# Retention and differential attention of block 1 in one run of 16 paired steps

## The reference

```python
scores = q @ k.T * 64 ** -0.5                       # retention, per head
dmask  = exp(lg_f * max(dist, 0)) * exp(lg_b * max(-dist, 0))
ret    = rms_norm((scores * dmask) @ v, g_ret) * silu(gate)
s      = q[m] @ k[m].T - slope[h] * abs(dist)       # differential, m = 0, 1
p      = softmax(s)
da     = rms_norm((p[0] - lam * p[1]) @ v, g_diff) * (1 - lam_init)
x      = x + concat(ret, da) @ w_out[l]
```

## Time and profile before

| | |
|---|---|
| median of 3 runs | 3374.51 us (3371.18 to 3377.08) |
| the profiled execution's own time | 3373.53 us |
| its span, first to last instruction | 3371.7 us |
| PE busy | 3133.2 us (93%) |
| PE weight loads | 2408.7 us (71%) |
| DVE busy | 1773.0 us (53%) |
| ACT busy | 1177.6 us (35%) |
| POOL busy | 1059.9 us (31%) |
| mean granted PE clock | 0.953 |

### The profile page before, as it was taken

The page is one execution under the profiler, slowest core; times in us unless marked ns, Lnnn a source line. Parts: engine busy times, 40 slices in busy tenths (PEclk is TensorE's granted clock), DMA queues, the critical chain, the costliest instruction groups (busy, mean ns, idle before and its releaser), DMA issues. The chain is left out here.

```text
span 3371.7 us, 45874 instructions
## 1 busy us (share of the span) xinstructions
PE 3133.2 (93%) x15912; PEld 2408.7 (71%) x15912; DVE 1773.0 (53%) x2788; ACT 1177.6 (35%) x1763; POOL 1059.9 (31%) x468
## 2 busy tenths in 40 slices
PE   7997699999999689999899898899999898899999
PEld 5842378887762268888678667788888676778787
DVE  4347764445436774445431674653354337657272
ACT  3224444233232535222222673332232225633231
POOL 3410144444330034444222313222223231144443
PEclk9988899999988789999999999999999898999999
DMA  4420034343340024444111001112122120023232
GB/s 147 148 80 0 23 124 150 127 151 111 126 140 0 0 89 148 131 148 133 50 50 56 29 28 50 44 62 75 50 65 72 43 69 21 1 81 101 86 99 94
DMA packets 72784, 270.06 MB, mean 80 GB/s; under 512 B 7920, under 2 KB 8944, under 8 KB 72560
## 3 DMA queue, kind: packets, MB, share of 16 engines
q1 hardware_dynamic: 71024, 264.34, 24.1%
q10 hardware_dynamic: 1664, 4.44, 0.4%
HBM read 266.65 MB, written 2.10 MB: 80 GB/s over the span
## 5 line engine op out<-in xcount | busy, mean ns | idle before, releaser
L524 POOL TENSOR_TENSOR w_lo<-w_raw,w_hi 128x1024 fp32r<-128x1024 f32 (+1 forms) x364 | 946.3, 2600 | 1559.9 <-ACT w_hi L1014 1559.9
L600 PE MATMUL ps<-h_hi,w_hi 128*128 128x512 f32 x3040 | 1040.7, 376 | 56.5 <-DVE h_lo L1530 29.5
L600 PE MATMUL ps<-h_lo,w_hi 128*128 128x512 f32 x3040 | 1025.8, 372 | 0.0
L600 PE MATMUL ps<-h_hi,w_lo 128*128 128x512 f32 x3040 | 1024.5, 371 | 0.0
L1014 ACT ACTIVATE w_hi<-w_raw 128x1024 fp32r<-128x1024 f32 (+1 forms) x364 | 406.4, 1117 | 1388.5 <-PE ps L600 1378.5
L600 PEld LDWEIGHTS ps<-h_hi,w_hi 128*128 128x128 f32 x3040 | 533.3, 190 | 188.9 <-issue 41.4
L600 PEld LDWEIGHTS ps<-h_hi,w_lo 128*128 128x128 f32 x3040 | 533.4, 191 | 100.6
L600 PEld LDWEIGHTS ps<-h_lo,w_hi 128*128 128x128 f32 x3040 | 534.3, 191 | 96.0 <-issue 0.5
L1659 DVE TENSOR_SCALAR conv_y<-u_pad,small 128x770 f32<-128x770 f32 (+1 forms) x88 | 176.2, 2002 | 196.8 <-ACT u_pad L1170 196.6
L1618 DVE SCALAR_TENSOR_TENSOR xT<-ps,mod,xT 128x512 f32 (+1 forms) x72 | 45.4, 659 | 309.9 <-PE ps L600 309.9
L1463 DVE CUSTOM_DVE_ANT_0 mod_junk<-mod_w,silu_c 128x1024 f32<-128x1024 f32 x96 | 140.8, 1467 | 121.7 <-DMA mod_w<-w_mod_dram 121.6
(11 more groups left out here) (192 smaller groups left out, 3488.4 us busy)
## 6 DMA issues: line engine op xcount, KB each, us to landing
mod_w<-w_mod_dram SPq DMA_DIRECT2D x96, 512.0 KB, 3.6
w_raw<-w_gu_dram SPq DMA_DIRECT2D x88, 512.0 KB, 3.5
w_raw<-w_down_dram SPq DMA_DIRECT2D x64, 704.0 KB, 4.1
w_raw<-w_up_dram SPq DMA_DIRECT2D x88, 512.0 KB, 3.4
w_raw<-w_in_dram SPq DMA_DIRECT2D x56, 512.0 KB, 3.5
w_raw<-na_qkv_dram SPq DMA_DIRECT2D x24, 512.0 KB, 3.5
w_raw<-w_out_dram SPq DMA_DIRECT2D x16, 512.0 KB, 3.5
w_raw<-swa_qkv_dram SPq DMA_DIRECT2D x12, 512.0 KB, 3.5
```

What stands on the lines that cost most here:

```text
L524: pool.tensor_tensor(w_lo[par][:, 0:cols], w_raw[par][:, 0:cols], w_hi[par][:, 0:cols].bitcast(F32), ALU.subtract).then_inc(w_lo_ready, 1)
L600: last = pe.matmul(acc[par][:, to:to + n], w[par][:, k * P:k * P + P], r[:, k, frm:frm + n], start=begin, stop=end)
```

## The change

The three phases become one, `mix`, of 16 steps s = 4 j + b over pair j and block b. Each step takes block b of both retention heads of pair j and query block b of differential head j. PE in step s scores the differential maps (banks 2, 3) and the retention heads (banks 0, 1), multiplies the retention values of s-1, turns s-2 and multiplies the differential values of s-3. The loops are unrolled, so q, k, v are read in `proj1` itself. The masks are made by three exponentials on ACT (384, 128 and 512 columns) and one product of 128 columns on POOL. DVE adds the bias and takes the minimum of the negated scores in one operation. Instead of dividing by both sums it forms e1 * lam * S0/S1 - e0, where e and S are a map's exponentials and their sum; the norm that follows cancels the remaining factor, if its epsilon is multiplied by S0 squared (`x_e2`) and the sign is turned in the gain. The squares and the gate product go to POOL. The means of all eight tiles are packed into few rows (`pack_tile`, 32 columns of weights), root and reciprocal are then taken of 128 x 128 twice in place of eight times 128 x 512, and `spread_tile` copies the rows back over the partitions by matmuls. The first `w_out` unit takes its tiles in the order 0, 1, 2, 4, 5, 3, 6, 7, with four of the spreads between its matmuls. The strip `d_dist` is loaded earlier, beside the other two, and some small buffers move to shared memory.

```diff
-        add("retention", layer=l)
-        add("diff", layer=l)
-        add("fin1", layer=l)
+        add("mix", layer=l)
...
-                    sp.dma_start(r_dpos[:], d["dist"][0]).then_inc(tab["retention"], 16)
-                    sp.dma_start(r_dneg[:], d["dist"][1]).then_inc(tab["retention"], 16)
+                    for n, strip in enumerate((r_dpos, r_dneg, d_dist)):
+                        sp.dma_start(strip[:], d["dist"][n]).then_inc(tab["mix"], 16)
...
+                def middle(j, hd):
+                    pool.wait_ge(x_strip, 8 * l + 2 * j + hd + 1)
+                    mask = r_mask[j % 2][hd][:, S - P:S]
+                    pool.tensor_tensor(mask, mask, r_mid[:, hd, :], ALU.mult).then_inc(x_mask, 1)
+
+                def square(n, tile, ready, count):
+                    pool.wait_ge(ready, count)
+                    if n >= 2:
+                        pool.wait_ge(f_sum, 32 * l + 4 * (n - 1))
+                    pool.tensor_tensor(f_sq[n % 2][:], proj1[:, tile, :], proj1[:, tile, :], ALU.mult
+                                       ).then_inc(f_sq_ready, 1)
+
+                def gate(j):
+                    pool.wait_ge(f_sq_ready, 7 * l + 2 * j + 1)
+                    pool.tensor_tensor(proj1[:, 8 + j, :], proj1[:, 8 + j, :], proj1[:, 24 + j, :], ALU.mult
+                                       ).then_inc(f_gated, 1)
...
+                def score_r(s):
+                    j, b = divmod(s, 4)
+                    if s:
+                        pe.wait_ge(x_masked, 32 * l + 2 * s)
+                    for hd, half in enumerate(halves_):
+                        pe.matmul(bank(hd), proj1[half, 12 + j, b * P:b * P + P], proj1[half, 8 + j, :],
+                                  start=True, stop=True).then_inc(x_scored, 1)
+
+                def score_d(s):
+                    j, b = divmod(s, 4)
+                    if s:
+                        pe.wait_ge(d_biased, 32 * l + 2 * s)
+                    for m, half in enumerate(halves_):
+                        pe.matmul(bank(2 + m), proj1[half, j, b * P:b * P + P], proj1[half, 4 + j, :],
+                                  start=True, stop=True).then_inc(d_scored, 1)
+
+                def values_r(s):
+                    j, b = divmod(s, 4)
+                    pe.wait_ge(x_masked, 32 * l + 2 * s + 2)
+                    if b == 0:
+                        pe.wait_ge(x_v_kept, 8 * l + 2 * j + 1)
+                        if j:
+                            pe.wait_ge(x_r_taken, 4 * l + j)
+                    for hd, half in enumerate(halves_):
+                        pe.matmul(bank(4)[half, :], r_vs[j % 2][:, b, half], r_sc[s % 2][:, hd, :],
+                                  start=(b == 0), stop=(b == 3)).then_inc(x_summed, 1)
...
+                    for c in range(4):
+                        last = pe.transpose(bank(6)[:, c * P:c * P + P], d_s[s % 3][:, 0, c * P:c * P + P], mat(IDENT))
+                    last.then_inc(d_turned, 1)
...
+                    for c in range(4):
+                        last = pe.matmul(bank(5)[:, b * P:b * P + P], d_vs[j % 2][:, c, :], d_aT[s % 2][:, c, :],
+                                         start=(c == 0), stop=(c == 3))
+                    last.then_inc(d_summed, 1)
...
+                    for g in range(4):
+                        last = pe.matmul(to[32 * g:32 * g + 32, 0:P], mats[:, PACKX, frm:frm + 32],
+                                         f_sq[n % 2][:, g * P:g * P + P], start=begin, stop=end and not which)
+                        if not which:
+                            last.then_inc(f_sum, 1)
+                    if which:
+                        pe.wait_ge(d_e2, 4 * l + j + 1)
+                        for g in range(4):
+                            pe.matmul(to[32 * g:32 * g + 32, 0:P], x_e2[j % 2][:, g, 14 - row:46 - row], mat(IDENT),
...
+                    for g in range(4):
+                        if which:
+                            at_ = 32 * g + row
+                            last = pe.matmul(to[:, g * P:g * P + P], mat(IDENT)[:, at_:at_ + 1].broadcast_to([P, P]),
+                                             x_rs[batch][:], start=True, stop=True)
+                        else:
+                            for hd, half in enumerate(halves_):
+                                at_ = 32 * g + row + hd
+                                last = pe.matmul(to[half, g * P:g * P + P],
+                                                 mat(IDENT)[:, at_:at_ + 1].broadcast_to([P, HD]),
...
+                turn_v(0)
+                turn_v(1)
+                for s in range(STEPS + 3):
+                    if s < STEPS:
+                        score_d(s)
+                        score_r(s)
+                    if 1 <= s <= STEPS:
+                        values_r(s - 1)
+                    if 2 <= s < STEPS + 2:
+                        turn_d(s - 2)
+                    if s >= 3:
+                        values_d(s - 3)
+                    if s < 12 and s % 4 >= 2:
+                        turn_v(2 * (s // 4) + s % 4)
+                    if s >= 6 and s % 2 == 0 and s < 18:
+                        pack_tile(s // 2 - 3)
+                for t in range(4):
+                    spread_tile(t)
+                pack_tile(6)
+                pack_tile(7)
+
+                def tail(at_):
+                    if at_ == 0:
+                        spread_tile(4)
+                    elif 2 <= at_ < 5:
+                        spread_tile(at_ + 3)
+                ends[0] = tail
 
             def na(ph):
...
+                    act.activation(mask[:, S:STRIP], r_dpos[:, S:STRIP], ACT.Exp, scale=lgam[:, at_:at_ + 1])
+                    act.activation(r_mid[:, hd, :], r_dpos[:, S - P:S], ACT.Exp, scale=lgam[:, at_:at_ + 1])
+                    act.activation(mask[:, 0:S], r_dneg[:, 0:S], ACT.Exp, scale=lgam[:, at_ + 8:at_ + 9]
+                                   ).then_inc(x_strip, 1)
...
+                for s in range(STEPS):
+                    j, o = divmod(s, 4)
+                    exp(s)
+                    if s >= 2:
+                        keep(s - 2)
+                    if o == 0 and j:
+                        take_r(j - 1)
+                    if o < 2 and j < 3:
+                        strip(j + 1, o)
+                    if o == 2 and j:
+                        take_d(j - 1)
+                    if o >= 2 and j < 3:
+                        keep_v(2 * j + o)
+                    if o == 3 and j < 3:
+                        bias(j + 1)
+                keep(14)
+                root(0)
+                keep(15)
+                take_r(3)
+                act.wait_ge(d_summed, STEPS * (l + 1))
+                act.wait_ge(f_sum, 32 * l + 24)
+                act.activation(f_sq[1][:], bank(5), ACT.Square).then_inc(f_sq_last, 1)
+                take_d(3)
                 hi(0)
-                square(5)
-                root(4)
-                hi(1)
-                square(6)
...
+                    for m in range(2):
+                        dve.wait_ge(d_scored, 32 * l + 2 * s + m + 1)
+                        dve.tensor_tensor_reduce(d_s[s % 3][:, m, :], bank(2 + m), d_bias[j % 2][:, (3 - b) * P:(3 - b) * P + S],
+                                                 -1.0, -NEG, ALU.add, ALU.min, x_min[:, s, m:m + 1]).then_inc(d_biased, 1)
...
+                    for hd in range(2):
+                        dve.wait_ge(x_mask, 8 * l + 2 * j + hd + 1)
+                        dve.wait_ge(x_scored, 32 * l + 2 * s + hd + 1)
+                        dve.scalar_tensor_tensor(out=r_sc[s % 2][:, hd, :], in0=bank(hd), scalar=HD ** -0.5,
+                                                 in1=r_mask[j % 2][hd][:, (3 - b) * P:(3 - b) * P + S],
+                                                 op0=ALU.mult, op1=ALU.mult).then_inc(x_masked, 1)
...
+                def probs(s):
+                    dve.wait_ge(d_exped, 32 * l + 2 * s + 2)
+                    dve.reciprocal(x_inv1[:, s:s + 1], x_sum[:, s, 1:2]).then_inc(d_scale, 1)
+                    dve.wait_ge(d_scale, 32 * l + 2 * s + 1)
+                    dve.scalar_tensor_tensor(out=x_ratio[:, s:s + 1], in0=x_inv1[:, s:s + 1], scalar=lam[:, 8 + l:9 + l],
+                                             in1=x_sum[:, s, 0:1], op0=ALU.mult, op1=ALU.mult).then_inc(d_scale, 1)
+                    dve.wait_ge(d_scale, 32 * l + 2 * s + 2)
+                    dve.scalar_tensor_tensor(out=d_s[s % 3][:, 0, :], in0=d_s[s % 3][:, 1, :], scalar=x_ratio[:, s:s + 1],
+                                             in1=d_s[s % 3][:, 0, :], op0=ALU.mult, op1=ALU.subtract).then_inc(d_probs, 1)
...
+                for s in range(STEPS + 1):
+                    if s < STEPS:
+                        scores(s)
+                        decay(s)
+                    if s:
+                        probs(s - 1)
+                    if s and s % 4 == 0:
+                        floor(s // 4 - 1)
+                invert(0)
```

(11 more changed lines are left out.)

659 lines of the change are left out of this document (239 added, 420 removed).

## The result

The changed kernel takes 3161.47 us (median of 4 runs, 3156.0 to 3162.59), the kernel before beside it 3374.73 (3371.18 to 3377.08): a ratio of 0.9366, 95% interval 0.9349 to 0.9382. It is faster by 213 us; I had forecast 169 and a lower bound of 3180. The direction was right, the size was not: the gain is 44 us larger than forecast, and the time fell out of the range.

What follows compares the result with a forecast made beforehand. PE was taken as the bound; 23.3 + 67 + 25 + 8 = 123 us a layer saves 169 from 3373.5, giving 3204.5, and with 0.3 for `mats` and 1.0 for the median 3206. Range 3180 to 3250.

Steps and rivals of the forecast that it cites:

- the rivals: Half clock 30 us, 0.08; DVE bound, 0.07; column pairs not overlapping, 0.04; half clock throughout, 0.03; steps one behind another, 0.02.
- the price of PE's work in a step: One step of the new stage on PE: two scores, retention values, turn and differential values, 4.9 us in all.
- (a): In each layer, from the last projection matmul to the end of step 3, with ACT the bound: 23.3 us.
- (b): Steps 4 to 15 of each layer: 12 x 4.9, `turn_v` 2.4, packs 3.0, and 5% added: 67 us.
- "four or five": Switches of tiling mode on PE in each step, estimated at 0.05 us each and left out of the sum.
- The 5% for hand-overs: Added to the 64.2 us of steps 4 to 15, as in `na`, making 67 us.
- (c): In each layer, from the end of step 15 to the end of the first `w_out` unit: 25 us.
- (d): The clock in each layer: 4 us for the start and 4 for the tail with its waits, 8 in all.
- The 4 us at the start: Allowance for the clock at the start of each layer's stage, where ACT is the bound anyway: 4 us.

## Why the prediction was wrong

The mechanism on record held in the main: PE is the bound, the pairs overlap by rows and by columns, and nothing outside the stage moved. None of the rivals came in this kernel. The step that failed is the price of PE's work in a step, 4.9 us for 4.41 measured; beside it stand three smaller terms, all put too high. The working gave 123 us a layer; measured are 102.0 and 100.8.

- **(a) 23.3, measured 22.9 and 21.7.** The number is right, but in part by luck. ACT sets the first wait (2.69 us for the first mask). It does not set the rest: in layer 0 it idles 1.47 us before the last exponentials ahead of `keep` and 0.29 before `keep` itself, the wait for `keep` is 0.8 us and not some 3, and taking the second pair's strips away changed nothing. What moved the end of step 3 was how long the clock stayed low.
- **(b) 67, measured 57.2.** 12 steps at 4.9 were 12 at 4.41 (5.9 us). The rows I priced from were each one matmul between changes of tiling (1.06), which is 0.86 for the matmul and 0.20 for a change. The new stage puts two score pairs of like tiling, and turn and values on the whole array, beside each other, and so has three changes in a plain step, not the "four or five" of the text. Two clues were in hand. The text weighed a change at 0.05 us and left it out, and never asked what part of the 1.06 was already such a change; and the kernel before had three value matmuls in a row, at 0.92 each. The `turn_v` and packs were another 1 us cheaper. The 5% for hand-overs (2.8 us) was read from a window of `na` where PE is busy 9.56 of 10; PE's wait in it (0.4 us) is for DVE, and the next window has DVE at 9.89 and PE at 8.66. It was a loss to another engine, not a toll of stepping. With PE the bound it is zero, 57.16 of 57.16.
- **(c) 25, measured 22.** Up to the unit PE took 10.3 us where 15.2 stood. I put root, high part, low part, product and the second reciprocal ahead of the unit (3.3 us), but the unit begins with tiles of the first batch and covers them; the rest is cheaper spreads, packs and values. The unit itself took 11.7 where 9.8 stood: waits of 0.8, and 0.87 us for a tile's three matmuls in place of 0.69. The term is near because the second error took back part of the first.
- **(d) 8, measured 0.** The 4 us at the start had been noted as lying under ACT, and were added all the same; what the low clock did cost there is inside the 22.9 of (a). In the tail the waits stayed under 0.7 us and the clock at 1.00.

That is 0.4 + 9.8 + 3 + 8 = 21.2 us in layer 0, where 21.0 are missing. The range failed for the same reason: its lower edge allowed 4.7 us a step with the hand-overs in it, and 6 us off in start and tail together, where (c) and (d) were 11 too high. Cautious terms that all have one sign are not an uncertainty, they are a shift.

**Where the gain of 213 comes from**, as far as runs separate it: one run of steps in place of two 51; the retention's pairs 24 + 25 (the second by layer 0, where the clock was like that of the kernel after); the alternation of single matmuls before, 13; the low clock of the retention before some 25, an estimate (30 us at half in each layer, which is 15 of work, against 6.8 and 3.4 us now). The rest, some 75, is the staging, the masks, the lighter DVE steps, the packed norm and the clock of `diff` and `fin1` together, which no run took apart; that clock was 0.76 in `diff` and is 1.00 in the new stage. Each part is the effect of one change alone, and that they add up is not shown.
